# Two transformer blocks on one core: 32 of the 256 tokens leave the dense expert matrices and take their experts row by row

## The chip, the core and the metric

One core of a Trainium2 chip runs the whole program as one launch. The metric is the device time in microseconds (us). The core has TensorE (PE in the profile, with its weight loads as PEld), VectorE (DVE), ScalarE (ACT), GpSimd (POOL) and the queue of SyncE (SP), which here only issues DMAs.

## The reference

The program computes two blocks on x of 256 tokens by 1024 columns, all in float32. The first block mixes a block attention and a latent attention, then has a dense MLP. The second block mixes a gated branch and a dilated attention. It ends with the part that the change is about, a mixture over 16,384 single-row experts:

```python
q = (xb @ w_query).reshape(128, 8, 2, 128)            # 8 heads, two half queries
s = jnp.einsum('thpc,pkc->thpk', q, sub_keys)         # 128 keys on each side
s1, i1 = lax.top_k(s[:, :, 0], 16); s2, i2 = lax.top_k(s[:, :, 1], 16)
cand = (s1[..., :, None] + s2[..., None, :]).reshape(128, 8, 256)
sc, ci = lax.top_k(cand, 16)
e = i1[ci // 16] * 128 + i2[ci % 16]                  # 8 x 16 = 128 experts of a token
g = softmax(sc)
act = gelu(einsum('td,thkd->thk', xb, expert_u[e]))
out = einsum('thk,thkd->td', g * act, expert_v[e])    # then x + out, and a final rms_norm
```

`expert_u` and `expert_v` are 16,384 by 1024 each, 64 MB each.

## The kernel before, in words

**Units.** All weights come as 421 units of 128 partitions by (mostly) 1024 columns, 512 KB each. SyncE loads unit u into a ring `raw` of NR = 4 (L2573). ScalarE rounds it to `whi` (L1209, float32r) and VectorE subtracts to get the rest, `wlo` = raw - whi (L1710, both inputs in SBUF). Eleven units named in LO_POOL, none of them an expert unit, have this subtraction on GpSimd (L2531). `whi` and `wlo` are rings of NH = 3. A product of float32 accuracy is three float32r matmuls: high by high, low by high, high by low. ScalarE may write unit u only when TensorE has used unit u - NH, and SyncE loads u + 4 only when `wlo` of u is made.

**The expert stage.** Instead of gathering, the kernel goes through all experts densely. Units EU to EU+127 are `expert_u`. For each one TensorE does `cols` (L535 to L542): 8 chunks by 3 products, the weight chunk of 128 columns as the loaded operand and the turned tokens `TH`, `TL` (256 columns) moving, so 24 matmuls of 256 columns. ScalarE takes a gelu of the result (L1636) into `stage`, and SyncE stores four of them at a time to DRAM (`acts`). In the first half of this stage VectorE finds the top 16 of every head (`route`, pulled piece by piece between its subtractions, up to n = TURN_AT = 67). From n = 69 on VectorE builds one-hot matrices for groups of four tokens: `one_hots` (L2430) has an is_equal (L2437) and a multiply (L2439), both with two SBUF inputs. TensorE multiplies them (`weigh`, L1122 to L1135, 8 matmuls of 128 float16 columns for a group, 64 groups), and ScalarE copies the result, the gate of each expert for each token, into the big tile ACTV (L1641). `hot_pair` spreads the groups over n = 69 to 127.

**The last stage.** Units EV to EV+127 are `expert_v`. For each, VectorE multiplies the gates by the fetched gelus (`take`, L2450), ScalarE rounds the product (`cut`, L1219), VectorE makes its low part (`cut`, L2454), both on 128 by 256 columns. `accumulate` (L1169 to L1172) then has the tokens as the loaded operand and the weights moving: 12 matmuls of 512 columns into four banks. After the last unit the sum is added to x, and the final norm and the stores follow (L2497 to L2525 on VectorE, L1684 on on ScalarE).

**Order.** Each engine's program is written out by hand, one instruction after the other. The engines meet only at semaphores, so an instruction that waits holds all that stands behind it on its engine. GpSimd (L2528) has thirteen subtractions and twelve DMAs in all and has nothing to do in the expert stages but one DMA for the final gain.

## Time and profile before

| | us |
|---|---|
| runs of the kernel before | 1254.0, 1254.1, 1253.54 (median 1254.0) |
| the profiled execution's own time | 1254.8 |
| its span, first to last instruction | 1253.0 |
| PE busy in the span | 1241.3 (99%) |
| DVE busy | 941.8 (75%) |
| ACT busy | 691.2 (55%) |
| POOL busy | 34.7 (3%) |

"Busy" is the union of the records of an engine, and matmuls are pipelined, so PE at 99% says that matmuls follow each other without a hole, not how dense each is. The page's slices show the `expert_u` stage from 523 to 898 us and the `expert_v` stage from 898.7 to 1247. The granted clock of TensorE is 1.00, its 2.4 GHz level, throughout.

### The profile page before, as it was taken

What the parts mean: (1) busy time and instruction counts of PE and PEld (TensorE: products, weight loads), DVE (VectorE), ACT (ScalarE), POOL (GpSimd) and SP (SyncE); (2) the same over time, 40 slices, a digit from 0 to 9 for tenths busy, and PEclk for the clock granted to TensorE, in tenths of its full rate; (3) what the DMA queues carried; (4) which work ended last, traced back from release to release, by engine and by line L of the source; (5) the groups of instructions that cost most, each with busy time, mean ns of one, the idle gap of its engine ahead of it and who ended that gap; (6) DMA issues with size and microseconds to landing.
All of it is one profiled execution on the core that took longest, in us unless ns stands there. A gap on an engine that the chain in (4) does not pass through costs nothing.

```text
span 1253.0 us, 21979 instructions
## 1 busy us (share of the span) xinstructions
PE 1241.3 (99%) x8585; PEld 1128.3 (90%) x8585; DVE 941.8 (75%) x1706; ACT 691.2 (55%) x1154; POOL 34.7 (3%) x29
## 2 busy tenths in 40 slices
PE   9999999999999999999999999999999999999998
PEld 8799989998878889999999999999988888888886
DVE  5886667764468767999999888888776767676766
ACT  5776467663465754454555555555645454545454
POOL 0000230000020010000000000000000000000000
PEclk9999999999999999999999999999999999999999
DMA  8444456666656445577777666666677766667663
GB/s 303 172 146 135 156 172 205 200 192 196 194 162 226 135 143 181 154 251 251 240 244 241 225 205 199 214 191 209 222 270 272 249 239 235 237 246 244 244 245 109
DMA packets 73127, 261.61 MB, mean 209 GB/s; under 512 B 8320, under 2 KB 8832, under 8 KB 72768
## 3 DMA queue, kind: packets, MB, share of 16 engines
q1 hardware_dynamic: 71552, 256.30, 61.7%
q0 software_dynamic: 1040, 3.34, 0.9%
q8 instruction: 69, 1.13, 0.4%
q10 hardware_dynamic: 432, 0.56, 0.1%
q14 instruction: 34, 0.28, 0.1%
HBM read 241.29 MB, written 18.87 MB: 208 GB/s over the span
## 4 chain that ended last, share of the span: by engine, by line
PE 94%; DVE 2%; DMA 1%; ACT 1%; POOL 1%; issue 0%; SPq 0%; DVEq 0%; ACTq 0%
PE ps L1172 27%; PE ps L532 15%; PE ps L540 15%; PE ps L541 14%; PE ps L542 14%; PE ps L1135 2%; DMA raw<-in_w_in_a_dram 1%; PE ps L577 1%; PE ps L590 1%; POOL wlo L2531 1%; PE ps L1094 1%; PE ps L607 1%; ACT whi L1209 1%; PE ps L599 0%; DMA raw<-in_w_in_q_dram 0%
## 5 line engine op out<-in xcount | busy, mean ns | idle before, releaser
L1209 ACT ACTIVATE whi<-raw 128x1024 fp32r<-128x1024 f32 (+2 forms) x420 | 441.9, 1053 | 433.8 <-PE ps L542 176.1
L1710 DVE TENSOR_TENSOR wlo<-raw,whi 128x1024 fp32r<-128x1024 f32 (+2 forms) x409 | 495.9, 1215 | 235.1 <-ACT whi L1209 232.6
L540 PE MATMUL ps<-turned_x,whi 128*128 128x256 f32 x1504 | 420.3, 279 | 0.0
L541 PE MATMUL ps<-turned_x,whi 128*128 128x256 f32 x1504 | 416.0, 277 | 0.0
L542 PE MATMUL ps<-turned_x,wlo 128*128 128x256 f32 x1504 | 415.9, 277 | 0.0
L1172 PE MATMUL ps<-whi,turned_x 128*128 128x512 f32 x1024 | 315.3, 389 | 0.0
L540 PEld LDWEIGHTS ps<-turned_x,whi 128*128 128x128 f32 x1504 | 282.6, 188 | 0.7 <-issue 0.5
L541 PEld LDWEIGHTS ps<-turned_x,whi 128*128 128x128 f32 x1504 | 282.9, 188 | 0.0
L542 PEld LDWEIGHTS ps<-turned_x,wlo 128*128 128x128 f32 x1504 | 282.4, 188 | 0.0
L1172 PEld LDWEIGHTS ps<-whi,turned_x 128*128 128x128 f32 x1024 | 192.2, 188 | 39.9 <-DVE wlo L1710 0.2
L1172 PE MATMUL ps<-wlo,turned_x 128*128 128x512 f32 x512 | 199.2, 389 | 0.0
L1172 PEld LDWEIGHTS ps<-wlo,turned_x 128*128 128x128 f32 x512 | 96.1, 188 | 20.1
L532 PE MATMUL ps<-whi,turned_x 128*128 128x512 f32 (+1 forms) x344 | 106.5, 386 | 2.6 <-DVE wlo L1710 2.6
L532 PEld LDWEIGHTS ps<-whi,turned_x 128*128 128x128 f32 x344 | 63.5, 188 | 16.8 <-DVE wlo L1710 4.3
L1641 ACT ACTIVATE ACTV<-ps 128x512 f32<-128x512 f32 x64 | 34.8, 595 | 55.3 <-PE ps L1135 55.3
L532 PE MATMUL ps<-wlo,turned_x 128*128 128x512 f32 (+1 forms) x172 | 63.5, 381 | 0.0
L2437 DVE TENSOR_TENSOR X<-keys,i 128x1024 f16<-128x1024 f16 x64 | 44.0, 687 | 16.4 <-PE ps L1135 16.4
L2450 DVE TENSOR_TENSOR ACTV<-ACTV,stage 128x256 f32<-128x256 f32 x128 | 53.3, 418 | 1.8 <-ACT ACTV L1641 1.8
L2454 DVE TENSOR_TENSOR turned_x<-ACTV,turned_x 128x256 fp32r<-128x256 f32 x128 | 53.4, 418 | 0.1
L1219 ACT ACTIVATE turned_x<-ACTV 128x256 fp32r<-128x256 f32 x128 | 51.1, 400 | 0.1
L532 PE MATMUL ps<-whi,MH 128*128 128x512 f32 x128 | 49.9, 390 | 0.0
L532 PE MATMUL ps<-whi,ML 128*128 128x512 f32 x128 | 49.8, 389 | 0.0
(350 smaller groups left out, 1208.0 us busy)
## 6 DMA issues: line engine op xcount, KB each, us to landing
raw<-in_expert_u_dram SPq DMA_DIRECT2D x128, 512.0 KB, 4.0
raw<-in_expert_v_dram SPq DMA_DIRECT2D x128, 512.0 KB, 3.7
raw<-in_w_up_dram SPq DMA_DIRECT2D x32, 512.0 KB, 4.3
raw<-in_w_down_dram SPq DMA_DIRECT2D x32, 512.0 KB, 3.6
acts<-stage SPq DMA_DIRECT2D x32, 512.0 KB, 4.2
stage<-acts SPq DMA_DIRECT2D x30, 512.0 KB, 3.3
raw<-in_w_in_dram SPq DMA_DIRECT2D x20, 512.0 KB, 3.8
raw<-in_w_gate_dram SPq DMA_DIRECT2D x16, 512.0 KB, 3.4
```

The lines of the kernel that those rows point to most:

```text
L532: m = e.matmul(o, x[:, k0 + j, sl], w[:, h, c:c + step], start=first, stop=last)
L540: e.matmul(dst, whi[:, h, sl], xh[:, k, :], start=k == 0, stop=False)
L541: e.matmul(dst, whi[:, h, sl], xl[:, k, :], start=False, stop=False)
L542: m = e.matmul(dst, wlo[:, h, sl], xh[:, k, :], start=False, stop=k == kn - 1)
L1172: m = e.matmul(ps[bank4(t, d)][:, :], x[:, n % 8, sl], w[:, h, d * 512:d * 512 + 512], start=n == 0 and k == 0, stop=n == 127 and k == 2)
L1209: e.activation(whi[:, u % NH, 0:n], raw[:, u % NR, 0:n], ACT.Copy).then_inc(*hi(u))
L1219: return e.activation(dst, src, ACT.Copy, scale=scale)
L1641: e.activation(ACTV[:, :, 4 * g:4 * g + 4], ps[g % 4][:, :].rearrange("p (t k) -> p k t", t=4), ACT.Copy, scale=1.0 / G_SCALE).then_inc(*w ...
L1710: e.tensor_tensor(wlo[:, u % NH, 0:n], raw[:, u % NR, 0:n], whi[:, u % NH, 0:n].bitcast(F32), ALU.subtract).then_inc(*lo(u))
L2437: e.tensor_tensor(made[:, 0:2, :, :, :], each_key, bc(i12[:, g, :, :, :], 3, 64), ALU.is_equal).then_inc(*hot_key(g))
L2450: e.tensor_tensor(ACTV[:, v, :], ACTV[:, v, :], stage[:, v % 8, :], ALU.mult).then_inc(*taken_v(i))
L2454: e.tensor_tensor(RL[:, i % 8, :], ACTV[:, V_ORDER[i], :], RH[:, i % 8, :].bitcast(F32), ALU.subtract).then_inc(*cut_d(i))
```

## The change

- `DENSE = 224`: the dense path holds tokens 0 to 223. Every expert matmul moves 224 columns. In the last stage the roles are swapped: the weight chunk is loaded and the tokens move, 24 matmuls of 224 columns for a unit in place of 12 of 512. Groups of one-hots fall from 64 to 56, four `weighed` in a row, with four buffers for them in place of two.
- The 32 tokens 224 to 255 are done by rows. Their 128 experts are laid out as 4 columns of 32 over the 128 partitions (partition = 32c + token, 32 rows each). Their numbers and gates go through small DRAM tensors. Then there are 32 rounds on `expert_u` rows, spaced 2.5 units apart from EU+72 on: GpSimd issues an indirect DMA of 128 rows (512 KB), multiplies the rows by x (128 by 1024, two SBUF inputs), and ScalarE sums them. 32 rounds on `expert_v` rows follow from EV+24 to EV+101, 2.5 units apart: GpSimd scales the rows by the weight of each partition and adds them to `held`. Two matmuls with a matrix of picks add the four partitions of a token, at n = 118 of the last stage, and VectorE adds the result to x.
- VectorE makes `wlo` of every expert unit, as before.
- `NH = 4`, with ScalarE's and VectorE's `split` one unit further ahead; in the first stage the angles, the order of some loads and the squares are moved.
- At the end the sums lie transposed, so each quarter is copied out of PSUM, turned by TensorE (`turn_end`, 16 transposes in all) and added.

```diff
-NH = 3
+NH = 4
+SCRATCH = 2048
+DENSE = 224
+GROUPS = DENSE // 4
+def rows_from(r):
+    return EU + 72 + 5 * r // 2 if r < 32 else EV + 24 + 5 * (r - 32) // 2
+def rows_summed(u):
+    return [r for r in range(32) if rows_from(r) + 3 == u]
...
-                m = cols(EU + n, 0, 8, TH, TL, ps[b][:, 0:256], range(4))
+                m = cols(EU + n, 0, 8, TH[:, :, 0:DENSE], TL[:, :, 0:DENSE], ps[b][:, 0:DENSE], range(4))
...
-            def accumulate(n, t, d):
-                h, sl = (EV + n) % NH, slice(t * 128, t * 128 + 128)
-                for k, (x, w) in enumerate(((RH, whi), (RH, wlo), (RL, whi))):
-                    m = e.matmul(ps[bank4(t, d)][:, :], x[:, n % 8, sl], w[:, h, d * 512:d * 512 + 512],
-                                 start=n == 0 and k == 0, stop=n == 127 and k == 2)
-                return m
+            def accumulate(n, c):
+                h, sl, dst = (EV + n) % NH, slice(c * 128, c * 128 + 128), ps[c // 2][:, c % 2 * 256:c % 2 * 256 + DENSE]
+                e.matmul(dst, whi[:, h, sl], TH[:, n % 8, 0:DENSE], start=n == 0 and c % 2 == 0, stop=False)
+                e.matmul(dst, whi[:, h, sl], TL[:, n % 8, 0:DENSE], start=False, stop=False)
+                return e.matmul(dst, wlo[:, h, sl], TH[:, n % 8, 0:DENSE], start=False, stop=n == 127 and c % 2 == 1)
+            def turn_end(b):
+                e.wait_ge(*(end_d if b % 2 else end_a).at(f"c{b}"))
...
+                for t in range(2):
+                    n = DENSE - 128 if t else 128
+                    for i in range(2):
+                        m = e.transpose(ps[4 + b % 2 * 2 + t][0:n, i * 128:i * 128 + 128], sums4[:, 2 * b + i, t * 128:t * 128 + n],
+                                        ident)
+                m.then_inc(*turned(f"end{b}"))
...
+                if n == 118:
+                    e.wait_ge(*row_p.at("sum31"))
...
+                    for d in range(2):
+                        m = e.matmul(ps[6 + d][:, :], picks, held[:, cols512(d)], start=True, stop=True)
+                    m.then_inc(*turned("rows"))
...
             def split(u):
+                if u == 3:
+                    split_one(3)
+                split_one(u + 1 if u >= 3 else u)
...
+            def dot_sum(r):
+                e.wait_ge(*row_p.at(f"made{r}"))
+                e.activation(made4, made4, ACT.Copy, accum_out=row_dot[:, r:r + 1]).then_inc(*row_a(f"dot{r}"))
...
+            def fetch_rows(r):
+                if r >= 64:
+                    return
+                e.wait_ge(*hi.at(rows_from(r)))
+                table, k = (A["expert_u_rows"], r) if r < 32 else (A["expert_v"], r - 32)
+                e.indirect_dma_start(out=row_ring[r % 2], out_offset=None, in_=table,
+                                     in_offset=bass.IndirectOffsetOnAxis(ap=row_at[:, k:k + 1], axis=0)).then_inc(*d_rows[r % 2](r))
...
+            e.tensor_scalar(held, held, row_r, None, ALU.mult).then_inc(*row_p("x"))
+            e.wait_ge(*row_p.at("x"))
+            e.tensor_tensor(held, held, made4, ALU.mult).then_inc(*row_p("gain"))
+            e.wait_ge(*row_p.at("gain"))
+            for r in range(32):
+                e.wait_ge(*d_rows[r % 2].at(r))
+                if r:
+                    e.wait_ge(*row_a.at(f"dot{r - 1}"))
+                e.tensor_tensor(made4, row_ring[r % 2], held, ALU.mult).then_inc(*row_p(f"made{r}"))
+                e.wait_ge(*row_p.at(f"made{r}"))
+                fetch_rows(r + 2)
...
+            for r in range(32):
+                e.wait_ge(*d_rows[r % 2].at(r + 32))
+                if r == 0:
+                    e.tensor_scalar(held, row_ring[0], row_act[:, 0:1], None, ALU.mult).then_inc(*row_p("sum0"))
+                else:
+                    e.tensor_scalar(row_ring[r % 2], row_ring[r % 2], row_act[:, r:r + 1], None, ALU.mult).then_inc(*row_p(f"scaled{r}"))
+                    e.wait_ge(*row_p.at(f"scaled{r}"))
+                    e.tensor_tensor(held, held, row_ring[r % 2], ALU.add).then_inc(*row_p(f"sum{r}"))
+                e.wait_ge(*row_p.at(f"sum{r}"))
+                fetch_rows(r + 34)
```

## Rows read from the trace of the kernel before

**Rows 1.** The page, part 1: busy us (share of the span) xinstructions.
```profile
PE 1241.3 (99%) x8585; PEld 1128.3 (90%) x8585; DVE 941.8 (75%) x1706; ACT 691.2 (55%) x1154; POOL 34.7 (3%) x29
```
**Rows 2.** Windows: us, busy us of PE, PEld, DVE, ACT, POOL, clock, DMA share, GB/s.
```profile
523.00:709.85 186.85, 186.85 (x1651) 186.81 (x1650) 174.28 (x373) 94.86 (x142) 0.00 (x0) 1.00 0.75 242
709.85:896.20 186.35, 186.35 (x1884) 185.25 (x1883) 150.92 (x183) 106.67 (x177) 0.00 (x0) 1.00 0.62 203
898.75:1246.95 348.20, 348.20 (x1538) 288.03 (x1536) 243.85 (x388) 176.47 (x262) 0.54 (x1) 1.00 0.67 237
20.00:30.00 10.00, 10.00 (x56) 8.91 (x55) 4.85 (x7) 5.43 (x9) 1.07 (x2) 1.00 0.98 371
```
**Rows 3.** Waits: engine line <- releaser: us in total, times, longest us.
```profile
ACT whi L1209 <- PE ps L1172: 169.0, 125, 1.4
```
**Rows 4.** Waits of PEld in 0 to 60 us.
```profile
PEld ps L532 <- DVE wlo L1710: 3.8, 4, 1.4
```
**Rows 5.** Timeline of PE at 600 us: start, us, engine, line, operation, forms.
```profile
600.03 0.28 PE L540 MATMUL ps<-turned_x,whi 128*128 128x256 f32 x1
...
602.98 0.28 PE L542 MATMUL ps<-turned_x,wlo 128*128 128x256 f32 x1
```
**Rows 6.** Timeline of PEld at 192 us and at 433 us.
```profile
192.07 0.30 PEld L900 LDWEIGHTS ps<-wlo,turned_x 128*128 128x128 f32 x2
192.30 0.19 PEld L540 LDWEIGHTS ps<-turned_x,whi 128*128 128x128 f32 x1
...
432.90 0.86 PEld L607 LDWEIGHTS ps<-v,PT 128*128 128x128 f32 x7
```
**Rows 7.** Timeline of DVE in expert_v and in the one-hot stretch.
```profile
1000.76 1.23 DVE L1710 TENSOR_TENSOR wlo<-raw,whi 128x1024 fp32r<-128x1024 f32 x1 [0.83 <-ACT whi L1209]
1001.90 0.42 DVE L2450 TENSOR_TENSOR ACTV<-ACTV,stage 128x256 f32<-128x256 f32 x1
1002.24 0.42 DVE L2454 TENSOR_TENSOR turned_x<-ACTV,turned_x 128x256 fp32r<-128x256 f32 x1
...
801.27 0.69 DVE L2437 TENSOR_TENSOR X<-keys,i 128x1024 f16<-128x1024 f16 x1 [0.66 <-PE ps L1135]
802.60 0.69 DVE L2437 TENSOR_TENSOR X<-keys,i 128x1024 f16<-128x1024 f16 x1
```
**Rows 8.** Timeline of POOL: its subtractions and a DMA that it issues.
```profile
22.47 0.54 POOL L2547 DMA_DIRECT2D gb<-in_g_post_mix_dram  x1
...
151.83 2.40 POOL L2531 TENSOR_TENSOR wlo<-raw,whi 128x1024 fp32r<-128x1024 f32 x1 [0.32 <-ACT whi L1209]
...
185.77 1.28 POOL L2531 TENSOR_TENSOR wlo<-raw,whi 128x512 fp32r<-128x512 f32 x1
...
360.35 5.27 POOL L2531 TENSOR_TENSOR wlo<-raw,whi 128x1024 fp32r<-128x1024 f32 x2 [168.53 <-ACT whi L1209]
```
**Rows 9.** L2067 by its source line (min/median/max ns), and DVE's timeline beside GpSimd.
```profile
L2067 DVE TENSOR_TENSOR st<-st x2: 159/466/774, 359.4 to 364.9; 128x1 f32<-128x1 f32 x2
...
364.86 0.77 DVE L2067 TENSOR_TENSOR st<-st 128x1 f32<-128x1 f32 x1
365.67 0.75 DVE L2073 SCALAR_TENSOR_TENSOR X<-tmp,st,X 128x512 f32<-128x512 f32 x1
...
186.75 0.85 DVE L2073 SCALAR_TENSOR_TENSOR X<-kv,st,X 128x512 f32<-128x512 f32 x1
```
**Rows 10.** Timeline of the end: PE, DVE, ACT.
```profile
1246.76 0.39 PE L1172 MATMUL ps<-whi,turned_x 128*128 128x512 f32 x1
...
1247.18 0.69 DVE L2499 TENSOR_TENSOR X<-X,ps 128x512 f32<-128x512 f32 x1
...
1247.90 0.63 ACT L1222 ACTIVATE raw<-X 128x512 f32<-128x512 f32 x1 [0.58 <-DVE X L2499]
...
1248.72 0.30 ACT L1694 ACTIVATE st<-st 128x1 f32<-128x1 f32 x1
1249.24 0.72 ACT L1219 ACTIVATE raw<-raw,st 128x512 f32<-128x512 f32 x1 [0.23 <-DVE st L2521]
```

More of the change, by code:

```diff
@@ L314, in build @@
         den, rden = stat(16), stat(16)
-        end_st = [(stat(2), stat(1), stat(1), stat(1)) for _ in range(2)]
+        end_part, end_tot, end_v, end_s, end_r = stat(8), stat(2), stat(2), stat(2), stat(2)
         class Heads:
@@ L384, in build @@
         d_out = [landing(f"out{i}") for i in range(4)]
+        d_rkept, d_listed, d_gated, d_at, d_gate, d_gain, d_picks = (
+            landing(n) for n in ("rkept", "listed", "gated", "at", "gate", "gain", "picks"))
+        d_held, d_scale = landing("held", range(4)), landing("scale", range(4))
+        d_rows = [landing(f"rows{i}", range(i, 64, 2)) for i in range(2)]
         used = signal("used", range(EV + 125))
@@ L505, in build @@
         score_d = signal("score_d", range(4))
-        hot_key = signal("hot_key", range(64))
-        hot = signal("hot", range(64))
+        hot_key = signal("hot_key", range(GROUPS))
+        hot = signal("hot", range(GROUPS))
         taken_v = signal("taken_v", range(128))
@@ L510, in build @@
         end_d = signal("end_d", (
-            "x00 x01 v0 g00 g01 r0 out01 x10 g10 x11 v1 g11 r1 out11").split())
+            "rows0 rows1 x00 x10 c1 x01 x11 x02 x12 c3 tot v x03 x13 g03 g13 r out01 out11").split())
+        row_p = signal("row_p", [
+            "x", "gain", *(f"made{r}" for r in range(32)), "act", "sum0", *(f"{w}{r}" for r in range(1, 32) for w in ("scaled", "sum")),
+            "g00", "g10", "g01", "g11", "g02", "g12"])
         def tensor_program(e):
@@ L1668, in scalar_program @@
                     take_u(n - 1)
+                for r in rows_summed(EU + n):
+                    dot_sum(r)
                 if n == TURN_AT:
@@ L1681, in scalar_program @@
                 split(EV + n + 2)
+                for r in rows_summed(EV + n):
+                    dot_sum(r)
+                if n == 30:
+                    e.wait_ge(*row_a.at("dot31"))
+                    e.activation(row_act, row_dot, ACT.Gelu_apprx_tanh).then_inc(*row_a("gelu"))
             cut(127)
@@ new lines, in end_sums @@
+            def end_sums(b):
+                e.wait_ge(*turned.at(f"end{b}"))
+                for t in range(2):
+                    xs = X[0:DENSE - 128 if t else 128, t, 256 * b:256 * b + 256]
+                    e.tensor_tensor(xs, xs, ps[4 + b % 2 * 2 + t][0:DENSE - 128 if t else 128, 0:256], ALU.add).then_inc(
+                        *end_d(f"x{t}{b}"))
+            e.wait_ge(*d_gb4.at(0))
+            end_sums(0)
+            take_sums(1)
+            end_sums(1)
+            end_sums(2)
@@ L2528, in pool_program @@
+            e.wait_ge(*end_a.at("s1"))
+            e.reciprocal(end_r, end_s).then_inc(*end_d("r"))
+            e.wait_ge(*end_d.at("r"))
+            e.wait_ge(*end_d.at("g13"))
+            for t in range(2):
+                e.wait_ge(*row_p.at(f"g{t}2"))
+                scaled_copy(fin[:, t, 512:1024], fin[:, t, 512:1024], end_r[:, t:t + 1]).then_inc(*end_d(f"out{t}1"))
         def pool_program(e):
@@ L2571, in sync_program @@
+            e.dma_start(picks, A["picks"]).then_inc(*d_picks(0))
+            e.wait_ge(*d_gb4.at(0))
+            e.wait_ge(*lo.at(UNITS - 1))
+            for b in range(3):
+                for t in range(2):
+                    e.wait_ge(*end_d.at(f"x{t}{b}"))
+                    e.tensor_tensor(fin[:, t, 256 * b:256 * b + 256], X[:, t, 256 * b:256 * b + 256], gb4[:, 256 * b:256 * b + 256],
+                                    ALU.mult).then_inc(*row_p(f"g{t}{b}"))
         def sync_program(e):
@@ L2734, in layouts @@
     d["sub_keys_2"] = i["sub_keys_2"][0].transpose(2, 0, 1)
+    d["expert_u_rows"] = i["expert_u_2"][0]
+    d["g_norm2"] = i["norm2_g_2"][0]
+    picks = np.zeros((128, 128), np.float32)
+    picks[np.arange(128), 96 + np.arange(128) % 32] = 1.0
+    d["picks"] = picks
     for n in ("g_post_mix", "g_post_mlp", "ln_v_g_2", "ln_v_b_2"):
```

313 lines of the change are left out of this document (195 added, 118 removed), and 1 row of the table turned.

## The prediction, written before the changed kernel was run

> **What bounds the kernel now.** I read the page's part 1 first. PE is busy in 99% of the span and DVE in 75% [rows 1]. Next come the windows by stage, since both expert stages together are 721 of the 1253 us [rows 2]: PE is without a hole in all three, while DVE is at 93% in the routing half, 81% in the one-hot half and 70% in `expert_v`. The waits say who leads: ScalarE waits for TensorE to free a slot of `whi`, 169.0 us in `expert_v` alone [rows 3], and VectorE's subtraction waits for ScalarE [rows 7]. So everybody waits for TensorE, and a change pays by what it takes from TensorE, as long as nobody else becomes later than TensorE.
>
> TensorE's pace: from 600.03 to 602.98 lie 26 matmuls of 256 columns, 113.4 ns each [rows 5], so 2.72 us for a unit of 24. In `expert_v`, 348.2 / 128 = 2.72 us too, for 12 matmuls of 512 columns, 226.7 ns each [rows 2]. That is 0.443 ns for a column in both. In the one-hot half 58 units take 186.35 us, 3.21 each. Less 58 x 2.72 this leaves 28.6 us for 64 groups, 0.45 us each.
>
> **TensorE with 224 columns.** No fp32r matmul with more than 128 and fewer than 256 columns is in the trace, so it must be bounded. By the columns it would be 224 x 0.443 = 99.2 ns. From above it is 113.4, no gain. What decides is the weight load, which every matmul has. Where the matmul is short, loads of 128 float32 columns still follow each other no closer than this: seven in a row over matmuls of 64 columns are (0.86 - 0.19) / 6 = 112 ns apart, and the float32r ones around L900, with 128 columns moving, start at 192.19 (the second of two) and 192.30, 110 ns apart [rows 6]. I take 112 ns: the load is just hidden under 256 columns and is the bound under 224. A unit is then 24 x 0.112 = 2.69 us, 0.03 less than now, where the columns promise 2.38.
>
> **GpSimd beside VectorE.** This is the step on which the forecast rests. L2067 is a sum over 128x1 elements with two SBUF inputs. It took 159 ns once and 774 ns the other time. The second starts at 364.86, inside GpSimd's pair of subtractions from 360.35 to 365.62, and ends at 365.63 [rows 8, 9]. L2073, also with two SBUF inputs, starts at 186.75 beside a GpSimd subtraction that ends at 187.05: it takes 0.85 in place of 0.75 us and ends 0.55 after GpSimd [rows 8, 9]. So a VectorE instruction with two SBUF inputs does not run beside a GpSimd instruction that reads SBUF; whoever comes second stands still until the other is done, with some 0.15 us of its start hidden. In both expert stages nearly all that VectorE does has two SBUF inputs: L1710, L2437, L2439, L2450, L2454. GpSimd has nothing there now. With the change it gets 34 instructions up to the last dot product and 63 in the sums. They are hidden only in the time that VectorE leaves free.
>
> GpSimd's prices: 2.40 us for two inputs of 1024 columns and 1.28 for 512 [rows 8], 2.19 ns a column, 0.16 fixed, so 2.24 us in which it holds VectorE up. Scaling with one tensor input is not in the trace. The ends are 0.98, twice the 0.49 us that VectorE needs for 512 columns of it, and 2.40, as for two inputs. I take 1.28, half the reads, with 1.12 of holding.
> The Trainium skill says (GPSIMD Engine Reference, Engine selection) that GpSimd's one-input operations run at roughly line rate; by that 1024 columns would be about 1.0 us and the 32 sums together some 9 us cheaper. No row here shows it.
>
> **The sum, stage by stage**, against the profiled execution's 1254.8 us:
>
> 1. First stages. PEld waits 3.8 us for VectorE's low halves [rows 4]. A fourth buffer and the angles moved ahead should remove most: -3 (bounds -4 and +3, as much again if the new order puts the wait elsewhere).
> 2. Routing half, 69 units: DVE needs 2.53 a unit, PE will need 2.69: 69 x -0.03 = -2 (bounds 0 and, with 99.2 ns, where DVE's 2.53 is next, -13).
> 3. One-hot half. TensorE: 2.69 + 56/58 x 0.45 = 3.12. VectorE: a group is 802.60 - 801.27 = 1.33, a subtraction 1.14 [rows 7], so 1.14 + 0.97 x 1.33 = 2.42 a unit, 6.06 in the 2.5 units of a round. GpSimd adds 2.24 less 0.15: 8.15 a round, 3.26 a unit. That is more than TensorE's 3.12, and 0.05 more than now: 56 units, +3 (bounds -5, if it fits into gaps, and +9, with nothing hidden). GpSimd's two preparations, 3.7 us, come once in the same place: +2 (0 to 4). Behind GpSimd's product stands ScalarE's `dot_sum`, and behind that the next `whi`; the lead of three units covers a few us of it.
> 4. `expert_v`, n = 0 to 23: VectorE 1.90 us a unit [rows 7], less 32 columns twice = 1.83, 4.57 a round, with 2.09 of GpSimd 6.66. TensorE needs 6.72. It just fits: -1.
> 5. `expert_v`, n = 24 to 103, 32 rounds of scale and add: 4.57 + 2.24 + 1.12 - 0.30 = 7.63 a round, 3.05 a unit against 2.72 now: 80 x 0.33 = +26. From below: VectorE holds only while data flow (1.53 a unit), 7.2 a round, +13; and -3 if nothing collides. From above: scaling as dear as adding and nothing hidden, 4.57 + 4.80 = 9.37 a round, +82. If VectorE won every race instead, GpSimd would fall behind and TensorE would wait for `sum31` at n = 118; the port time is the same, only the place differs.
> 6. n = 104 to 127: -1. Two matmuls of 512 for the picks, +1.
> 7. The end. From the last matmul (1246.76) to the end are 6.2 us now [rows 10]. Added on the path: 12 transposes at 0.112 before the last matmuls, 1.3; then a copy of 448 columns 0.6 (512 are 0.69), four transposes with their latency 0.8, a second square root 0.3, a second copy on ScalarE 0.7 with its DMA issue, less 0.2 for squares of 256: +3.8 (2 to 6).
>
> Sum: -3 - 2 + 3 + 2 - 1 + 26 - 1 + 1 + 3.8 = +29 over 1254.8, 1284; the profiled run stands 0.8 over the median of 1254.0, so **1283 us**. By its own bounds this case reaches from 1258 to 1340.
>
> DMA: a unit in step 4 moves 524 KB, 115 KB of gelus and 210 KB of rows, 849 KB in 2.69 us, 316 GB/s. The trace has 371 GB/s over 10 us [rows 2], so it costs nothing. At 3.05 us it is 278.
>
> **Rivals.** (A) *No collision that counts*: GpSimd's work falls into VectorE's gaps (0.83 us a unit now, [rows 7]) or the two run side by side. For it: GpSimd's subtraction at 151.83 took 2.40 us beside busy VectorE instructions, but those had an input in PSUM. Against it: L2067. Then step 3 is -5, step 5 -3, the preparations 0: 1254.8 - 10, **1244**, faster. It decides where the holding per round stays under 6.72 - 4.57 = 2.15 us; I have 3.4.
>
> (B) *The columns count and nothing collides*: 99.2 ns a matmul. Step 2 -13, step 3 58 x (2.81 - 3.21) = -23, `expert_v` 128 x (2.38 - 2.72) = -43, ends as above: **1176**. It needs 849 KB in 2.38 us, 357 GB/s, close under the 371 seen. Against it rows 6.
> The Trainium skill (TensorE: Matmul & The Clock Gate, Back-to-back issue gap) gives columns / 2.4 + 2.5 ns for back-to-back matmuls, 95.8 ns for 224; at 256 it gives 109.2 and the trace has 113.4, at 128 float32 columns 55.8 where the loads in rows 6 are 110 apart. By that rule the time is this rival's.
>
> (C) *The columns count, but the port binds*: step 5 stays, steps 2 and 6 gain 13 and 8: **1264**.
>
> (D) *GpSimd's own chain is the bound*: scale, add and an indirect issue, each waited for. A plain issue is 0.54 us [rows 8]; an indirect one is not in the trace, and 128 row addresses may cost several times that. 94 units of 2.69 us for 32 rounds are 7.9 us; scale, add and two waits for VectorE take about 5.5, so from 2.4 us an issue on, TensorE stands at n = 118. At 4 us: 32 x 9.5 - 253 = +51, with the rest some **1310**.
>
> **Chances.** Forecast 0.60, A 0.13, B 0.07, C 0.08, D 0.12. The range for 8 in 10 is 1243 to 1330: it takes in A and C, and of the forecast all but its dearest corner. What a measurement here can tell from no change is about 0.2%, 2.5 us. Slower than that: nearly all of the forecast and D, most of C, 0.76; faster: A and B, 0.19; same 0.05.
>
> **What the profile after would show.** PE's matmuls of 224 columns 112 ns apart (99 would be B or C). Windows: `expert_v` n = 24 to 103 at 3.05 us a unit against 2.69 in its last 20 units; PE or PEld waiting for `wlo`, tens of us in total, where now there is none. L1710 and the one-hots longer than 1.23 and 0.69 us on average, and GpSimd's products longer than 2.40, each ending when the other's ends. Wrong would be: L1710 at its 1.22 us beside GpSimd's work, a unit under 2.72 us in that stretch, or one long wait at n = 118.

## The result: slower, twice as far as forecast

The changed kernel takes 1314.7 us (median of 4 runs, 1311.2 to 1320.0), the kernel before 1254.05 us beside it: ratio 1.0486, 95% interval 1.0471 to 1.0501. The forecast was 1283 us, within 1243 to 1330. The direction was right, the size was not: +61 us where +29 stood. The profiled execution of the changed kernel took 1311.2 us, its span is 1309.2.

The page after, part 1 [rows 1]:

```profile
PE 1250.9 (96%) x10077; PEld 1192.9 (91%) x10077; DVE 1092.6 (83%) x1696; ACT 716.5 (55%) x1220; POOL 414.6 (32%) x212
```

PE stands for 4.5% of the span now (0.9% before), GpSimd went from 3% to 32%. The chain of work that ended last, 94% PE's before, runs for a third over VectorE (shares by engine, then by line):

```profile
PE 56%; DVE 35%; DMA 5%; ACT 2%; issue 1%; SPq 0%; DVEq 0%; ACTq 0%
```

Windows of the changed kernel, columns as in [rows 2]: routing half, one-hot half, `expert_v` n = 0 to 23, n = 24 to 103, n = 104 to 123, the end.

```profile
514.50:701.90 187.40, 187.40 (x1681) 187.40 (x1680) 177.67 (x395) 95.48 (x144) 6.68 (x13) 1.00 0.70 235
709.90:897.25 187.35, 179.22 (x1795) 177.35 (x1793) 183.66 (x166) 123.14 (x213) 95.83 (x47) 0.99 0.75 257
897.25:962.70 65.45, 64.67 (x579) 64.50 (x578) 57.95 (x70) 39.91 (x66) 40.56 (x18) 1.00 0.83 312
962.70:1232.80 270.10, 233.04 (x1922) 228.09 (x1921) 253.19 (x241) 111.81 (x167) 226.66 (x96) 0.96 0.72 256
1232.80:1288.50 55.70, 55.58 (x484) 54.47 (x485) 42.03 (x67) 28.87 (x43) 4.42 (x3) 1.00 0.63 224
1288.50:1309.20 20.70, 12.87 (x114) 12.43 (x113) 8.37 (x21) 9.14 (x26) 4.28 (x6) 0.87 0.14 51
```

The same stages before, by the starts of the same units, took 190.4, 181.6, 65.3, 217.6, 54.4 and 16.95 us; `expert_u` starts 2.2 us earlier, and three units between the halves take 8.0 instead of 10.0. Of the span's +56.2 us, +52.5 lie in n = 24 to 103, in which the 32 rounds of scaling and adding run: 3.377 us a unit, 2.720 before. GpSimd is busy there in 226.7 of 270.1 us. Its groups over the whole run, by form (count | busy, mean ns | idle before):

```profile
L2752 POOL TENSOR_SCALAR ACTV<-ACTV,stage 128x1024 f32<-128x1024 f32 x31 | 91.4, 2948 | 2.0 <-DMA ACTV<-in_expert_v_dram,stage 0.7
L2738 POOL TENSOR_TENSOR ACTV<-ACTV 128x1024 f32<-128x1024 f32 x32 | 88.6, 2767 | 57.9 <-ACT ACTV L1719 57.8
L2754 POOL TENSOR_TENSOR ACTV<-ACTV 128x1024 f32<-128x1024 f32 x31 | 75.3, 2428 | 2.6
L2722 POOL DMA_INDIRECT ACTV<-in_expert_v_dram,stage x32 | 57.7, 1803 | 22.5 <-ACT whi L1285 14.0 <-POOL ACTV L2754 7.9 <-POOL ACTV L2750 0.3
```

VectorE's groups in 962.7 to 1232.8 (L1821 makes the low half, L2568 weighs, L2572 cuts), and TensorE's wait there:

```profile
L1821 DVE TENSOR_TENSOR wlo<-raw,whi 128x1024 fp32r<-128x1024 f32 x81 | 160.0, 1975 | 18.5 <-ACT whi L1285 18.5
L2572 DVE TENSOR_TENSOR turned_x<-ACTV,turned_x 128x224 fp32r<-128x224 f32 x80 | 76.7, 959 | 0.0
L2568 DVE TENSOR_TENSOR ACTV<-ACTV,stage 128x224 f32<-128x224 f32 x80 | 35.8, 447 | 0.0
```
```profile
PE ps L1224 <- DVE turned_x L2572: 35.1, 22, 1.8
```

Undisturbed, these three take 1.21, 0.38 and 0.38 us. How they are stretched shows in DVE's timeline, and below it POOL's for the same round:

```profile
1087.27 3.42 DVE L1821 TENSOR_TENSOR wlo<-raw,whi 128x1024 fp32r<-128x1024 f32 x1
1090.61 0.38 DVE L2568 TENSOR_TENSOR ACTV<-ACTV,stage 128x224 f32<-128x224 f32 x1
1090.91 2.07 DVE L2572 TENSOR_TENSOR turned_x<-ACTV,turned_x 128x224 fp32r<-128x224 f32 x1
1092.91 1.21 DVE L1821 TENSOR_TENSOR wlo<-raw,whi 128x1024 fp32r<-128x1024 f32 x1
1094.04 0.38 DVE L2568 TENSOR_TENSOR ACTV<-ACTV,stage 128x224 f32<-128x224 f32 x1
1094.34 0.38 DVE L2572 TENSOR_TENSOR turned_x<-ACTV,turned_x 128x224 fp32r<-128x224 f32 x1
1094.65 3.42 DVE L1821 TENSOR_TENSOR wlo<-raw,whi 128x1024 fp32r<-128x1024 f32 x1
```
```profile
1087.18 2.42 POOL L2754 TENSOR_TENSOR ACTV<-ACTV 128x1024 f32<-128x1024 f32 x1
1089.88 1.69 POOL L2722 DMA_INDIRECT ACTV<-in_expert_v_dram,stage  x1 [0.27 <-POOL ACTV L2754]
1091.61 2.87 POOL L2752 TENSOR_SCALAR ACTV<-ACTV,stage 128x1024 f32<-128x1024 f32 x1
1094.56 2.42 POOL L2754 TENSOR_TENSOR ACTV<-ACTV 128x1024 f32<-128x1024 f32 x1
```

The low half that starts beside the adding stands 2.2 us (3.42 less 1.21). The cut at 1090.91 stands 1.7 us: from 0.7 us ahead of the scaling's start until about 1.0 us of it have passed (its own 0.38 us counted last). After that VectorE runs at full speed, though the scaling lasts until 1094.48. I call the excess of such an instruction over its undisturbed time a block, and put it down to the GpSimd instructions it overlaps. In n = 24 to 103 there are 30 blocks by an adding, 2.2 us each, 24 by an issue and the scaling behind it, 1.70 each, and 5 by a scaling alone, 0.86 each.

### The profile page after: what moved, and what is told of

It is laid out like the page before. It is cut to its first block, busy times and chain, and to the rows that moved or that the text cites. A ratio compares the mean times of both kernels' runs of the same rounds, so it can differ in the third digit from the quotient of the medians.

```text
span 1309.2 us, 25300 instructions
## 1 busy us (share of the span) xinstructions
PE 1250.9 (96%) x10077; PEld 1192.9 (91%) x10077; DVE 1092.6 (83%) x1696; ACT 716.5 (55%) x1220; POOL 414.6 (32%) x212
## 4 chain that ended last, share of the span: by engine, by line
PE 56%; DVE 35%; DMA 5%; ACT 2%; issue 1%; SPq 0%; DVEq 0%; ACTq 0%
DVE wlo L1821 18%; PE ps L585 14%; PE ps L593 10%; PE ps L595 10%; PE ps L594 10%; DVE turned_x L2572 5%; DMA raw<-in_expert_v_dram 4%; DVE ACTV L2568 3%; DVE more_room L2557 2%; PE ps L1224 2%; PE ps L1225 2%; PE ps L1226 2%; DVE X L2555 2%; DVE more_room L2555 2%; ACT whi L1285 2%; DVE X L2557 1%
## 5 line engine op out<-in xcount | busy, mean ns | idle before, releaser
L1821 DVE TENSOR_TENSOR wlo<-raw,whi 128x1024 fp32r<-128x1024 f32 (+2 forms) x409 | 574.8, 1410 | 147.0 <-ACT whi L1285 144.4
L593 PE MATMUL ps<-turned_x,whi 128*128 128x224 f32 (+1 forms) x1504 | 417.7, 278 | 0.0
L594 PE MATMUL ps<-turned_x,whi 128*128 128x224 f32 (+1 forms) x1504 | 415.0, 276 | 0.0
L595 PE MATMUL ps<-turned_x,wlo 128*128 128x224 f32 (+1 forms) x1504 | 415.0, 276 | 0.0
L1224 PE MATMUL ps<-turned_x,whi 128*128 128x224 f32 x1024 | 289.4, 283 | 38.0 <-DVE turned_x L2572 36.8
L593 PEld LDWEIGHTS ps<-turned_x,whi 128*128 128x128 f32 x1504 | 287.7, 191 | 0.7 <-issue 0.5
L594 PEld LDWEIGHTS ps<-turned_x,whi 128*128 128x128 f32 x1504 | 287.7, 191 | 0.0
L595 PEld LDWEIGHTS ps<-turned_x,wlo 128*128 128x128 f32 x1504 | 287.5, 191 | 0.0
L1225 PE MATMUL ps<-turned_x,whi 128*128 128x224 f32 x1024 | 286.4, 280 | 0.0
L1226 PE MATMUL ps<-turned_x,wlo 128*128 128x224 f32 x1024 | 286.2, 280 | 0.0
L1224 PEld LDWEIGHTS ps<-turned_x,whi 128*128 128x128 f32 x1024 | 201.6, 197 | 43.5 <-issue 40.5
L1226 PEld LDWEIGHTS ps<-turned_x,wlo 128*128 128x128 f32 x1024 | 201.9, 197 | 0.0
L1225 PEld LDWEIGHTS ps<-turned_x,whi 128*128 128x128 f32 x1024 | 201.7, 197 | 0.2 <-issue 0.2
L2738 POOL TENSOR_TENSOR ACTV<-ACTV 128x1024 f32<-128x1024 f32 x32 | 88.6, 2767 | 57.9 <-ACT ACTV L1719 57.8
L2572 DVE TENSOR_TENSOR turned_x<-ACTV,turned_x 128x224 fp32r<-128x224 f32 x128 | 101.8, 795 | 0.2 <-ACT turned_x L1295 0.2
L2752 POOL TENSOR_SCALAR ACTV<-ACTV,stage 128x1024 f32<-128x1024 f32 x31 | 91.4, 2948 | 2.0 <-DMA ACTV<-in_expert_v_dram,stage 0.7
L2754 POOL TENSOR_TENSOR ACTV<-ACTV 128x1024 f32<-128x1024 f32 x31 | 75.3, 2428 | 2.6
L585 PEld LDWEIGHTS ps<-whi,turned_x 128*128 128x128 f32 x344 | 63.5, 188 | 12.5 <-issue 0.7
```

The lines of the kernel that those rows point to most:

```text
L585: m = e.matmul(o, x[:, k0 + j, sl], w[:, h, c:c + step], start=first, stop=last)
L593: e.matmul(dst, whi[:, h, sl], xh[:, k, :], start=k == 0, stop=False)
L594: e.matmul(dst, whi[:, h, sl], xl[:, k, :], start=False, stop=False)
L595: m = e.matmul(dst, wlo[:, h, sl], xh[:, k, :], start=False, stop=k == kn - 1)
L1224: e.matmul(dst, whi[:, h, sl], TH[:, n % 8, 0:DENSE], start=n == 0 and c % 2 == 0, stop=False)
L1225: e.matmul(dst, whi[:, h, sl], TL[:, n % 8, 0:DENSE], start=False, stop=False)
```

## The experiments

Each ratio is to the kernel before, run beside it, with its 95% interval; "changed" is the changed kernel.

**1. e1_no_rows**: the changed kernel without anything for the 32 tokens.

```
-  x4.p1 route0 route1 route2 rows end0 end1
+  x4.p1 route0 route1 route2 end0 end1
...
-            fetch_rows(0)
-            fetch_rows(1)
...
-            for r in range(32):     # products; sums: likewise
```

> The changed kernel without any work for the 32 tokens (no lists, gathers, products, sums or picks; their expert output is left out). It shows what the dense part with 224 columns is worth by itself. Theory (weight load bounds a matmul at 111 to 112 ns, everything lost is lost to the rows): 1243 us, from 1240 to 1248, so at most 1% under the kernel before; expert_v 2.69 us a unit throughout. If the 224 columns counted in full with the rows gone, 1180.

1241.3 us, 0.989 (0.986 to 0.992), inside the 1240 to 1248 expected. So the dense part is worth some 12 us at most; experiment 10 says how much of that is due to the other parts of the change.

**2. e2_narrow_arith**: gathers whole, products, scalings and addings on 1 column.

```
-                e.tensor_tensor(made4, row_ring[r % 2], held, ALU.mult)
+                e.tensor_tensor(made4[:, 0:1], row_ring[r % 2][:, 0:1], held[:, 0:1], ALU.mult)
...
-                    e.tensor_scalar(row_ring[r % 2], row_ring[r % 2], row_act[:, r:r + 1], None, ALU.mult)
-                    e.tensor_tensor(held, held, row_ring[r % 2], ALU.add)
+                    e.tensor_scalar(row_ring[r % 2][:, 0:1], row_ring[r % 2][:, 0:1], row_act[:, r:r + 1], None, ALU.mult)
+                    e.tensor_tensor(held[:, 0:1], held[:, 0:1], row_ring[r % 2][:, 0:1], ALU.add)
```

> All gathers, waits and ScalarE's sums stay, but GpSimd's products, scalings and additions of the rounds work on 1 column in place of 1024 (the row results are left out by that). Theory A (GpSimd reading SBUF stops VectorE's two-input instructions): almost all of the loss goes, 1250 us, from 1244 to 1260; what stays is up to 0.5 us for each indirect issue. Theory B (the gathered 33 MB make the unit loads late): the loss stays, 1300 or more. Theory C (GpSimd's own chain of 7.4 us a round paces the stage): also gone, 1245 to 1250.

1247.1 us, 0.994 (0.992 to 0.996). The 64 gathers alone cost 5.8 us over e1, and the kernel stays under the one before. All the rest, 67.6 us, hangs on the columns of GpSimd's arithmetic. The low half beside the issues is undisturbed (DVE, 962.7 to 1232.8):

```profile
L1821 DVE TENSOR_TENSOR wlo<-raw,whi 128x1024 fp32r<-128x1024 f32 x99 | 122.0, 1232 | 89.5 <-ACT whi L1285 89.2
```

**3. e3_no_gather**: the arithmetic stays, only the first two gathers are made.

```
                 e.wait_ge(*hi.at(rows_from(r)))
+                if r > 1:
+                    return
...                              # and no waits for the landing of the other 62
```

> GpSimd's products, scalings and additions stay at full width, but of the 64 gathers only the first two are made (the rounds work on old rows). Theory A (port): most of the loss stays, 1295 us, from 1285 to 1305; per round the 2.2 us for two inputs and 1.1 for scaling stay, the 0.5 of the indirect issue goes. Theory B (DMA): loss gone, 1250. Theory C (GpSimd's chain): round of 5.4 in place of 7.4 us, so it would fall under TensorE's 6.7 and the loss would be gone too, 1250.

1282.95 us, 1.022 (1.019 to 1.026): 32 us under the changed kernel and 12 under the 1295 expected, just outside its range. So the 62 issues or their bytes, 5.8 us by themselves, cost 32 beside the arithmetic. n = 24 to 103 takes 244.0 us. Its 32 blocks by a scaling alone are 0.84 us each, half of those behind an issue.

**4. e6_gp_kinds**: the kernel before with ten GpSimd instructions of each of four kinds in `expert_v`, on buffers that nobody uses.

```
+            for r in range(40):
+                e.wait_ge(*hi.at(EV + 8 + 5 * r // 2))
+                ...  # 10 products, 10 scalings by a column, 10 by a constant, 10 memsets
```

> The kernel before, with 40 instructions on GpSimd in expert_v, one in 2.5 units, on a tile of its own: ten products of two SBUF inputs, ten scalings by a per-partition scalar, ten by a constant, ten memsets, each 128 by 1024. Port theory: VectorE's longest instruction beside a product goes from 1.22 to about 3.4 us, beside a scaling to about 2.3 (GpSimd needs 2.9 us but reads only for 1.1), beside a memset it stays at 1.22. Whole run 1254 to 1258. If GpSimd held VectorE for the whole of its instruction, beside a scaling it would be 4.1; if it never did, 1.22 throughout.

1253.6 us. The rows, POOL first and then DVE:

```profile
975.15 2.64 POOL L2577 TENSOR_TENSOR gp_room<-gp_room 128x1024 f32<-128x1024 f32 x1 [2.03 <-ACT whi L1211]
983.36 4.04 POOL L2579 TENSOR_SCALAR gp_room<-gp_room 128x1024 f32<-128x1024 f32 x1 [5.57 <-ACT whi L1211]
...
1064.92 3.74 POOL L2581 TENSOR_SCALAR gp_room<-gp_room 128x1024 f32<-128x1024 f32 x1 [4.42 <-ACT whi L1211]
...
1119.29 0.96 POOL L2583 MEMSET gp_room<- 128x1024 f32 x1 [4.39 <-ACT whi L1211]
```
```profile
975.47 3.41 DVE L1712 TENSOR_TENSOR wlo<-raw,whi 128x1024 fp32r<-128x1024 f32 x1
...
983.20 1.22 DVE L1712 TENSOR_TENSOR wlo<-raw,whi 128x1024 fp32r<-128x1024 f32 x1
984.35 0.42 DVE L2452 TENSOR_TENSOR ACTV<-ACTV,stage 128x256 f32<-128x256 f32 x1
984.68 1.26 DVE L2456 TENSOR_TENSOR turned_x<-ACTV,turned_x 128x256 fp32r<-128x256 f32 x1
985.92 1.23 DVE L1712 TENSOR_TENSOR wlo<-raw,whi 128x1024 fp32r<-128x1024 f32 x1
```

The product stops the low half for 2.2 us. The scaling at 983.36 first stands behind the running low half (4.04 us instead of 2.9), then stops VectorE for 0.84 us only, where 1.1 was expected: the cut ends at 985.94, and the next low half takes its 1.23 us while the scaling goes on until 987.40. A memset stops nobody. In this kernel VectorE has room for 2.2 us in the 6.8 us of a round, and TensorE does not stand once in `expert_v`, so the time does not move. (It is a single run.)

**5. e9_gp_filler**: as e3, with 1.6 us of memsets in each round where the issue stood.

```
                 e.wait_ge(*row_p.at(f"sum{r}"))
+                e.memset(made4, 0.0)
+                e.memset(made4[:, 0:640], 0.0)
                 fetch_rows(r + 34)
```

> The changed kernel with only the first two indirect gathers (as in e3_no_gather, 1282.95 us), and with two memsets of a buffer that nobody reads then (1024 and 640 columns, some 1.6 us together by the 0.96 us of one of 1024 columns) in each of the 32 summing rounds, where the indirect issue stood. It leaves out the gathers; the sums are of stale rows. A memset left VectorE's halves at 1.22 us in e6_gp_kinds, so it holds VectorE off nowhere; it only makes GpSimd's chain of a round as long as it was with the issue (about 7.4 us). Theory 'chain' (the 32 us between 1314.7 and 1283.0 come from the length of GpSimd's chain, with which VectorE falls in step, two units a round): 1305 to 1316 us. Theory 'issue' (they come from the time in which an indirect issue itself keeps VectorE from SBUF): 1281 to 1286 us. In between: both.

1286.3 us, 1.023 (1.019 to 1.027). A GpSimd chain as long as with the issues brings back 3 us of the 32, so "chain" falls. The total hides two changes, though: n = 24 to 103 takes 229.8 us, 14 less than in e3, as the later rounds have moved behind the stage, and TensorE then stands 13.5 us at n = 118 for `sum31`. So what the added length costs shows at n = 118 and not in the stage.

**6. e4_narrow_scaling**: scalings on 1 column, the rest as changed.

```
-                    e.tensor_scalar(row_ring[r % 2], row_ring[r % 2], row_act[:, r:r + 1], None, ALU.mult)
+                    e.tensor_scalar(row_ring[r % 2][:, 0:1], row_ring[r % 2][:, 0:1], row_act[:, r:r + 1], None, ALU.mult)
```

> The changed kernel with its 31 scalings on 1 column instead of 1024; the 32 gathers, products and addings stay whole. It leaves out the scaling of 1023 columns. Scaling lasts 2.95 us and holds VectorE off for about 1.1. Theory 'holding only' (each us held is paid, nothing else): 31 x 1.1 = 34 less than 1314.7, so 1281 us. Theory 'chain': GpSimd's round falls from 7.4 to about 4.5 us, under the 6.8 us of TensorE's 2.5 units; VectorE needs 2.5 x 1.73 + 2.2 (adding) + 0.5 (issue) = 7.0 us a round against 6.8, so 1247.1 (narrow arithmetic) + 32 x 0.2 = 1254 us, with 1250 to 1262 as the range. Rival 'scaling is free since it overlaps': over 1300 us.

1281.6 us, 1.020 (1.016 to 1.024): 33 us less, 1.07 for each of 31 scalings. "Holding only" had the number (1281), but by luck: in the changed kernel the blocks with a scaling in them are mostly 1.70 us, not 1.1, and over n = 24 to 127 all blocks together fall from 115 us to 46, so twice as much block went as time. My reckoning by VectorE's average room (1254) was wrong too. In 960 to 1225 TensorE has ten stops of over 0.25 us, and within the 8 us ahead of each of them ScalarE had waited 2.4 to 5.5 us for raw weights. The waits of e4 in 960 to 1225 (SPq is SyncE's queue of DMA issues; L2791 fetches four units' gelus into `stage`):

```profile
ACT whi L1285 <- DMA raw<-in_expert_v_dram: 89.5, 42, 5.5
SPq L2791 <- DVE ACTV L2568: 155.8, 24, 9.2
PE ps L1224 <- DVE turned_x L2572: 11.6, 16, 1.4
```

Late loads alone do not stop TensorE: in e2 ScalarE waits 114.2 us for them and no stop is over 0.5 us. Blocks of 2.2 us alone do not either (e6). In e4 both meet. Which of the two could be taken away with more profit, no run says.

**7. e5_scaling_on_act**: the scalings on ScalarE; GpSimd adds and issues.

```
+                for r in range(32):
+                    if n == 32 + 5 * r // 2:
+                        e.wait_ge(*d_rows[r % 2].at(r + 32))
+                        e.activation(row_ring[r % 2] if r else held, row_ring[r % 2], ACT.Copy,
+                                     scale=row_act[:, r:r + 1]).then_inc(*row_a(f"scaled{r}"))
```

> The changed kernel with all 32 scalings of gathered expert_v rows moved from GpSimd to ScalarE (Copy with a scale per partition, before the cut of every 2.5th unit from n = 32); GpSimd only adds and issues. Everything is computed. ScalarE is 55% busy and has about 1 us of room in a unit of 2.7 us. If the scalings on GpSimd are what overloads the sum, this comes to the time of e4_narrow_scaling plus what the ScalarE instructions cost: 1254 to 1262 us. If ScalarE's readings of SBUF hold VectorE off as GpSimd's do, or its queue delays the high halves, 1275 us or more.

1296.1 us, 1.032 (1.028 to 1.037). ScalarE scales in 1.14 us and holds VectorE off nowhere: every block (25 of 2.20 us) is an adding's. But the adding now starts on ScalarE's signal, nearly always just as VectorE begins the weighing (28 of 29 blocks are on that line), on which ScalarE's cut and TensorE wait; in e4 many addings met VectorE only in part, and its blocks of n = 24 to 127 came to 46 us, here to 64. TensorE's waits for the low cut (L2572 of the changed kernel, L2579 here) come to 23.0 us instead of 11.6. Late loads have a part in it here too (ScalarE waits 77.9 us for them; the longest stop, 3.92 us, follows such a wait of 5.25), and as the two longest stops end TensorE's clock is at the 1.2 GHz level, for 6.83 us each time. So 14 of the 33 us are lost again. The expectation had 1275 or more only for ScalarE's reads or its queue; the reads hold nobody, and what the queue alone costs is not separated.

**8. e7_half_columns**: the kernel before, `expert_u` with 128 moving columns.

```
-                m = cols(EU + n, 0, 8, TH, TL, ps[b][:, 0:256], range(4))
+                m = cols(EU + n, 0, 8, TH[:, :, 0:128], TL[:, :, 0:128], ps[b][:, 0:128], range(4))
...                                                           # chunks 4 to 7 likewise
```

> The kernel before with its expert_u matmuls on 128 moving columns instead of 256 (tokens 128 to 255 left out of expert_u). The forecast took a floor of one weight load, 110 to 112 ns, under a matmul of 224 columns. By the floor: spacing 109 to 112 ns instead of 113.4, the 69 units of the first half about 187 us instead of 190, the whole 1244 to 1250 us. By columns alone: spacing near 57 ns, VectorE or ScalarE bound near 1.8 us a unit, the whole under 1190 us.

1247.5 us, inside the 1244 to 1250 expected. The same window of it and of e1_no_rows, with 128 and 224 columns:

```profile
520.00:705.00 185.00, 185.00 (x1659) 185.00 (x1659) 175.01 (x382) 96.55 (x144) 0.00 (x0) 1.00 0.76 243
```
```profile
520.00:705.00 185.00, 185.00 (x1659) 185.00 (x1658) 175.29 (x375) 93.83 (x143) 0.00 (x0) 1.00 0.69 237
```

1659 matmuls in both, 111.5 ns each with the routing's transposes; 256 columns fit 1634 into 185 us, 113.2 ns. A matmul of 128 columns costs as much as one of 224, so the floor is something that every matmul has whatever its columns. That it is the weight load is argued from the loads' spacing of 110 to 112 ns in [rows 6]; no run changes the load alone.

**9. e10_thin_gather**: all 64 issues, 1/16 of the bytes.

```
+                w = 1024 if r < 2 else 64
-                e.indirect_dma_start(out=row_ring[r % 2], out_offset=None, in_=table,
+                e.indirect_dma_start(out=row_ring[r % 2][:, 0:w], out_offset=None,
+                                     in_=table.rearrange("a (b d) -> (a b) d", d=w),
```

> The changed kernel with all 64 indirect gathers, but from the third on each brings 64 elements of a row instead of 1024 (32 KB in place of 512 KB, and rows of other addresses; the sums are of other numbers). Products, scalings and addings keep their 1024 columns. It tells apart what a gather costs by its issue on GpSimd and what it costs by its bytes: without issues and bytes the kernel took 1282.95 us (e3_no_gather), with both 1314.7. Theory 'issue' (VectorE is kept from SBUF while GpSimd issues, 0.54 us each by the blocks counted in the two traces): the 17 us that these blocks come to stay, so 1300 to 1310 us. Theory 'bytes' (the loads of expert weights land later beside a gather, 6.5 to 7 us instead of 3.5, and the raw buffer that VectorE frees late can't make up for it): 1281 to 1288 us. Both by the counted parts: 1300 us.

1310.1 us, 1.045 (1.043 to 1.046). Of the 32 us the issues cost 27, the bytes 4.6. There are 28 blocks by an issue with a scaling behind it, 1.71 us each.

**10. e8_dense_tuned**: the kernel before with the change's buffers, order and scratch, 256 tokens.

```
-NH = 3
+NH = 4
...
+                split_one(u + 1 if u >= 3 else u)
```

> The kernel before with the parts of the change that have nothing to do with the 32 tokens: four high-half buffers, the halves made a unit further ahead, the order of the first stages, the smaller DMA scratch. All 256 tokens stay in the expert matrices; everything is computed. First stages: -2.2 us as in the changed kernel, the rest as before: 1250 to 1253 us, ratio 0.997 to 1.000. If the 13 us between the kernel before and e1_no_rows (1241.3) came from these parts and not from the 224 columns, it would be near 1241 us.

1253.4 us, 0.9993 (0.9984 to 1.0002): no difference. From here to e1 it is 12.1 us, by what goes with 224 tokens: by the profiled executions the routing half is 2.9 us shorter, the one-hot half 7.9 (with 56 groups in place of 64), `expert_v` up to n = 103 3.8, and the rest with the new end is 2.9 longer.

**11. e11_gap_after_issue**: a memset of 0.98 us between each issue and the next scaling.

```
             for r in range(32):
                 e.wait_ge(*d_rows[r % 2].at(r + 32))
+                e.memset(made4, 0.0).then_inc(*row_p(f"pad{r}"))
+                e.wait_ge(*row_p.at(f"pad{r}"))
```

> The changed kernel with one memset (1024 columns of a buffer that nobody reads then, 0.96 us) between each indirect issue and the scaling that follows it, 32 of them. Everything is computed. e10_thin_gather showed that the 64 issues cost 27 us by themselves, and in the traces a block of VectorE that covers an issue and the scaling behind it lasts 1.71 us (24 times in the changed kernel, 28 in e10_thin_gather), a block by a scaling without an issue ahead 0.84 us (32 times in e3_no_gather). Theory 'tail' (an issue keeps VectorE from SBUF in its own last part): the blocks at the issue stay, so 1308 to 1318 us. Theory 'pair' (only an issue with a SBUF instruction straight behind it does, as with the narrow arithmetic of e2_narrow_arith, where issues blocked nothing): 31 x 0.86 = 27 less, so 1286 to 1292 us. The 1 us more in GpSimd's chain costs at most the 4 us that the filler of e9_gp_filler did.

1321.4 us, 1.053 (1.052 to 1.055): outside both, and the total alone would have said "tail". The stage says the opposite: n = 24 to 103 takes 218.9 us instead of 268.5 (from low half to low half), no block covers an issue with its scaling any more, and the 18 by scalings are 0.78 us in the mean. But a GpSimd round is now 9.9 us, the rounds run past the stage, and TensorE stands at n = 118 for `sum31` (waits of PE and PEld, 1200 to 1300):

```profile
PEld ps L1254 <- issue: 52.0, 3, 51.0
```

That is the forecast's rival D, brought about by a pad.

**12. e12_issue_before_add**: three row buffers in the sum; the issue stands between scaling and adding.

```
+                    fetch_rows(r + 34)
                     e.tensor_tensor(held, held, row, ALU.add).then_inc(*row_p(f"sum{r}"))
                 e.wait_ge(*row_p.at(f"sum{r}"))
-                fetch_rows(r + 34)
```

> The changed kernel with three row buffers in the sum (the products' buffer is free then), so that each round's issue stands between its scaling and its adding instead of between an adding and the next scaling. Everything is computed. Theory 'tail': the issue's hold comes before the adding's instead of before the scaling's, same price: 1308 to 1318 us. Theory 'scaling behind an issue' (only that order is dear): up to 27 less, 1286 to 1295 us; if an adding behind an issue is as dear as a scaling, again 1308 to 1318 us.

1301.7 us, 1.038 (1.036 to 1.040), between the theories. Scalings block 0.84 again, and where VectorE meets the issue with the adding behind it (15 times) the block is 2.97 us in place of 2.20. So an adding straight behind an issue is as dear as a scaling there. 13 us came back: about half of the issues now met nobody, and the blocks of n = 24 to 127 fell by 9 us, from 115 to 106; the other 4 are not traced.

**13 and 14. e13_short_gap, e14_middle_gap**: as e11, memsets of 64 and of 384 columns.

```
-                e.memset(made4, 0.0).then_inc(*row_p(f"pad{r}"))
+                e.memset(made4[:, 0:64], 0.0).then_inc(*row_p(f"pad{r}"))
```

> As e11_gap_after_issue with memsets of 64 columns in place of 1024 (some 0.1 us by the 0.96 us of 1024, or as much as an instruction costs at least). In e11 no VectorE instruction was stretched by an issue with its scaling behind (blocks in n = 24 to 103: adding 2.20, scaling 0.78 us), but GpSimd's round grew to 9.9 us, so that TensorE waited 51 us at n = 118 for the last sum. Theory 'pair, any instruction in between breaks it': GpSimd's round stays near 7.8 us, no wait at n = 118, blocks 3.0 instead of 3.46 us a round, so 1286 to 1296 us. Theory 'time since the issue decides' (the issue is not over when its record ends): the block of an issue with its scaling stays at about 1.7 less 0.1 us, so 1308 to 1314 us.

> As e13_short_gap with memsets of 384 columns (about 0.4 us). 'Pair': 1290 to 1300 us, GpSimd's round 0.3 us longer than in e13. 'Time since the issue': the block shrinks to about 1.3 us, 1296 to 1306 us and less than e13.

1289.9 us, 1.029 (1.025 to 1.033), and 1299.5 us, 1.036 (1.033 to 1.039). Both are where "pair" had them. One added instruction of 0.18 us per round makes the changed kernel 24.8 us faster. The blocks by a scaling are 0.77 us in the mean in e13 and 0.83 in e14. Over n = 24 to 127 all blocks fall from 115 to 80 us in e13: 21 of these 36 us are the extra hold behind the issues, the others come from addings that now meet VectorE less often or only in part. So the 25 us are not the pair's price alone. A longer gap helps no more and costs GpSimd's time (n = 104 to 127: 71.8 and 78.1 us; 62.1 in the changed kernel). A round of e13, DVE and POOL:

```profile
1090.24 1.21 DVE L1821 TENSOR_TENSOR wlo<-raw,whi 128x1024 fp32r<-128x1024 f32 x1
1091.38 0.38 DVE L2568 TENSOR_TENSOR ACTV<-ACTV,stage 128x224 f32<-128x224 f32 x1
1091.68 1.22 DVE L2572 TENSOR_TENSOR turned_x<-ACTV,turned_x 128x224 fp32r<-128x224 f32 x1
1092.83 1.21 DVE L1821 TENSOR_TENSOR wlo<-raw,whi 128x1024 fp32r<-128x1024 f32 x1
```
```profile
1088.60 2.00 POOL L2722 DMA_INDIRECT ACTV<-in_expert_v_dram,stage  x1 [0.27 <-POOL ACTV L2756]
1090.59 0.18 POOL L2749 MEMSET ACTV<- 128x64 f32 x1
1090.87 3.53 POOL L2754 TENSOR_SCALAR ACTV<-ACTV,stage 128x1024 f32<-128x1024 f32 x1
```

With the memset between, VectorE's low half of 1090.24 gets through beside the end of the issue, and the scaling waits for it; without it VectorE stands from before the scaling's start.

## Why the prediction was wrong

**Step 5 failed, by the size of its block term and by a term that was missing.** It said 4.57 + 2.24 + 1.12 - 0.30 = 7.63 us a round, +26; measured is +52.5. The forecast's 244 us for the stage are 146.4 of VectorE's own work and 97.9 of blocks. The measured 270.1 us are:

- VectorE's own work 1.73 us a unit, 138.6 us: 8 less than forecast.
- Blocks: 253.2 busy less 138.6, so 114.6 us, 3.58 a round; forecast 3.06. The adding was right (2.2). The scaling alone blocks 0.84, not 1.12, though it lasts 2.95 us, not 1.28: the two errors were in opposite directions, and only the blocking counts. What was missing is that an instruction straight behind an indirect issue blocks 0.86 us more (24 x 0.86 = 20.6 us). I had priced the issue as GpSimd's time only, in rival D. e10 (27 us by issues) and e13 (24.8 back by a 0.18 us instruction) show it. Without issues (e3) the stage takes 244.0, the forecast's number, but by luck: there the blocks are 93.0 and VectorE's holes 10.9, and its own work is 6 less than forecast.
- VectorE idle, 16.9 us; forecast none. These are five holes, and at each of them ScalarE had waited 3.4 to 5.9 us for a load of raw weights. SyncE issues in order, and its fetch of four units' gelus waits until VectorE has done the fourth `take`; the next four weight loads stand behind it and then go out together. The queue waited so for 135.7 us in 960 to 1225, for 65.0 in the kernel before. 10.7 of the 16.9 us lie before 999 us. There they cost little: the sums begin not at n = 24 but only when ScalarE has made the gelu at n = 30 (GpSimd waits 18.6 us for it), and until then TensorE sets the pace, with two stops of 1.4 and 1.5 us. The other 6.2 are the holes at 1150 and 1217 us. The gathers' bytes are 4.6 us in all (e10), so "DMA costs nothing" was nearly right as to the rate; the order of the queue was not in the forecast, and no run changes it.

```profile
976.28 1.06 ACT L1285 ACTIVATE whi<-raw 128x1024 fp32r<-128x1024 f32 x1 [5.93 <-DMA raw<-in_expert_v_dram]
1151.91 1.06 ACT L1285 ACTIVATE whi<-raw 128x1024 fp32r<-128x1024 f32 x1 [3.65 <-DMA raw<-in_expert_v_dram]
SPq L2791 <- DVE ACTV L2568: 135.7, 19, 8.9
```

The range did hold 1314.7, but its upper bound stood on a scaling that holds VectorE as long as an adding, and it holds 0.84 us against 2.2: luck. The reach given for this case, 1258 to 1340, is also narrower than its bounds added up, which go to 1357.

**What held.** The floor: 112 ns forecast, 111.5 measured (187.40 us for 1681 matmuls), the same for 128 and 224 columns (e7), and the routing half -3.0 us against -2. That rejects B and C. The formula of the Trainium skill (TensorE: Matmul & The Clock Gate, Back-to-back issue gap), 95.8 ns for 224 columns, does not hold here. The same section says itself that the formula has no budget for the weight loads and counts too little where the columns are few, which the prediction left out; that sentence the runs bear out. The port: e2 against the changed kernel (67.6 us by the columns of GpSimd's arithmetic) rejects A. The first stages: -2.2 (-3). The one-hot half with its preparations +5.7 (+5) at 3.345 us a unit (3.26), and -2.0 for the three units between the halves, for which the forecast had no term of its own. n = 0 to 23: +0.1 (-1). The rest of `expert_v` +1.3 (0), the end +3.7 (+3.8). Rival D did not occur in the changed kernel: no wait at n = 118. But its condition was nearly met, since GpSimd was busy for 226.7 of 270.1 us, and e11 went over it.

The Trainium skill (GPSIMD Engine Reference, Engine selection) has one-input operations at roughly line rate, by the prediction's estimate about 1.0 us here. The scaling took 2.95 us, more than an adding with its two inputs (2.43); the measurement decides. Its blocking, 0.84 us, is near that figure; no run shows that this is more than chance. The Trainium skill also says that a VectorE instruction with two SBUF inputs and a GpSimd one that reads SBUF lock each other out of a shared port for the whole instruction (SBUF — State Buffer, SBUF: two separate sides). For the product e6 agrees, and for the adding the changed kernel (2.2 us of 2.4); for the scaling e6 does not (0.84 of 2.9).

**Prices, by whole runs.** 224 instead of 256 tokens in the dense path, with the end that goes with it: -12.1 us (e8 to e1). 64 gathers: +5.8 (e2). The arithmetic's columns: +67.6, and of these the scalings 33 (e4), a memset between issue and scaling 25 (e13), the two not independent. The work taken from TensorE was worth 12 us, and no run that keeps GpSimd's addings whole (1281.6 at best, with the scaling left out; 1289.9 with everything computed) comes near 1254. No version with rows that beats the kernel before and computes everything was found.

## What to carry to other kernels

Price a GpSimd instruction beside a busy VectorE by how long it stops VectorE, not by how long it runs, and measure that on an idle buffer in the kernel at hand, as experiment 4 does. See what stands straight behind an indirect DMA issue: a short instruction without SBUF inputs there bought back 25 of 61 us. Look at what stands ahead of the weight loads in their queue once another engine sets the pace; that is advice from the trace, not from a run. And before cutting the moving columns of fp32r matmuls, look at how close matmuls of fewer columns already follow each other in the trace: here, under 111.5 ns, fewer columns are worth nothing.
